# Latent attention: the order of turns, scores and root rows around the last gate tile

## The reference, cut to what matters

```python
yc = gla_mixer(gq, gk, gv, g_low, gr, ...)      # gated linear attention, 4 heads of 128
#   o = rms_norm(o, g_norm);  return o * silu(gr)
yd = mla_mixer(c_q, c_kv, k_r, ...)             # latent attention, 4 heads, causal, blocks of 128 queries
#   s = (q_nope k_nope + q_rope k_rope) * scale;  masked;  p = softmax(s);  o = p v
y = concatenate([yc, yd]) @ od_w_out
x = layer_norm(ALPHA * x + y, ...)
```

## Time and profile before

| | us |
| --- | --- |
| median of 3 runs | 2010.84 |
| lowest, highest | 2009.81, 2011.89 |
| profiled execution, its own time | 2011.19 |
| span of the profiled execution | 2009.4 |
| TensorE matmuls busy | 1965.6 (98% of the span) |
| VectorE, ScalarE, GpSimd busy | 935.4, 733.3, 344.2 |
| mean granted TensorE clock | 0.993 |

### The profile page before, as it was taken

How to read it: one execution, slowest core, us unless ns; L and a number is a source line. 1 busy time by engine, 2 the same in 40 slices (tenths; PEclk the granted TensorE clock), 3 DMA queues, 4 the chain that set the end, 5 groups by cost and what they waited for, 6 DMA issues and landing times.

```text
span 2009.4 us, 27314 instructions
## 1 busy us (share of the span) xinstructions
PE 1965.6 (98%) x11541; PEld 1188.6 (59%) x11541; DVE 935.4 (47%) x1254; ACT 733.3 (36%) x1173; POOL 344.2 (17%) x355
## 2 busy tenths in 40 slices
PE   8999999999999999999999999999999999999997
PEld 5655655757664444885568444448865585444476
DVE  6666686655543322244655222223555663222224
ACT  6444312445343431143534232212464543322213
POOL 1011111410132210033014121100400124212001
PEclk9999999999999999999999999999999999999999
DMA  7221200233322333322121232334111123322331
GB/s 245 84 84 60 68 22 21 87 123 105 105 69 100 105 105 105 106 85 103 59 97 59 89 102 103 105 105 137 53 64 45 40 85 105 104 88 101 105 105 43
DMA packets 28228, 179.66 MB, mean 89 GB/s; under 512 B 2960, under 2 KB 7184, under 8 KB 7184
## 3 DMA queue, kind: packets, MB, share of 16 engines
q1 hardware_dynamic: 27312, 170.93, 24.7%
q10 hardware_dynamic: 512, 4.94, 0.7%
q0 software_dynamic: 288, 2.10, 0.3%
HBM read 175.86 MB, written 2.10 MB: 89 GB/s over the span
## 4 chain that ended last, share of the span: by engine, by line
PE 90%; DVE 5%; ACT 2%; issue 1%; DMA 1%; POOL 1%; SPq 0%; ACTq 0%; DVEq 0%
PE psum_a L383 26%; PE psum_a L385 26%; PE psum_a L384 26%; PE psum_b L520 2%; PE psum_a L724 2%; PE psum_a L662 1%; DMA W<-weights 1%; DVE ARENA L1831 1%; PE psum_b L639 1%; PE psum_a L735 1%; ACT W_PARTS L1238 1%; PE psum_b L1063 1%; DVE W_PARTS L1812 1%; PE psum_a L704 1%; PE psum_a L851 1%
## 5 line engine op out<-in xcount | busy, mean ns | idle before, releaser
L1812 DVE SCALAR_TENSOR_TENSOR W_PARTS<-W,W_PARTS 128x2048 f16<-128x2048 f32 x138 | 316.1, 2294 | 583.6 <-ACT W_PARTS L1238 583.6
L383 PE MATMUL psum_a<-U,W_PARTS 128*128 128x512 f16 (+1 forms) x1240 | 465.9, 376 | 2.8 <-DVE U L1826 1.8
L384 PE MATMUL psum_a<-U,W_PARTS 128*128 128x512 f16 (+1 forms) x1240 | 465.7, 376 | 0.0
L385 PE MATMUL psum_a<-U,W_PARTS 128*128 128x512 f16 (+1 forms) x1240 | 465.5, 375 | 0.0
L1238 ACT ACTIVATE W_PARTS<-W 128x2048 f16<-128x2048 f32 x138 | 262.3, 1905 | 441.9 <-PE psum_a L385 440.1
L383 PE MATMUL psum_a<-ARENA,W_PARTS 128*128 128x256 f16 (+1 forms) x860 | 268.6, 312 | 1.9 <-DVE ARENA L2327 1.3
L385 PE MATMUL psum_a<-ARENA,W_PARTS 128*128 128x256 f16 (+1 forms) x860 | 268.6, 312 | 0.0
L384 PE MATMUL psum_a<-ARENA,W_PARTS 128*128 128x256 f16 (+1 forms) x860 | 268.6, 312 | 0.0
L383 PEld LDWEIGHTS psum_a<-U,W_PARTS 128*128 128x128 f16 x1240 | 121.5, 98 | 148.7 <-issue 5.1
L385 PEld LDWEIGHTS psum_a<-U,W_PARTS 128*128 128x128 f16 x1240 | 121.5, 98 | 141.8 <-issue 0.8
L384 PEld LDWEIGHTS psum_a<-U,W_PARTS 128*128 128x128 f16 x1240 | 121.5, 98 | 141.4 <-issue 3.5
(11 more groups left out here) (316 smaller groups left out, 2966.3 us busy)
## 6 DMA issues: line engine op xcount, KB each, us to landing
W<-weights SPq DMA_DIRECT2D x159, 1024.0 KB, 4.8
CON<-const ACTq DMA_DIRECT2D x1, 3071.5 KB, 11.2
X<-x_in SPq DMA_DIRECT2D x4, 256.0 KB, 3.8
X<-x_in SPq DMA_DIRECT2D x1, 1024.0 KB, 8.0
U<-dft POOLq DMA_DIRECT2D x1, 1024.0 KB, 5.3
ARENA<-dft POOLq DMA_DIRECT2D x1, 1024.0 KB, 5.2
U<-mem_in ACTq DMA_DIRECT2D x1, 1024.0 KB, 4.7
y_out<-U SPq DMA_DIRECT2D x2, 512.0 KB, 2.9
```

The costliest lines, as they stand in the source:

```text
L383: nc.tensor.matmul(out, left(0), right(0), start=first, stop=False)
L384: nc.tensor.matmul(out, left(0), right(1), start=False, stop=False)
L385: return nc.tensor.matmul(out, left(1), right(0), start=False, stop=last)
L1812: nc.vector.scalar_tensor_tensor(out=home[:, 1, :], in0=W[g % 2][:, :], scalar=W_SCALE, in1=home[:, 0, :], op0=ALU.mult, op1=ALU.subtract) ...
```

## The change

On TensorE the turns of block 1 and the scores of block 3 move into `gr1_after`, so that they stand ahead of the last gate tile. The root rows of heads 0 to 2 stand right behind that tile, then the turns of block 2, and the root row of head 3 behind those; `head_roots` gets the heads as a list for this. On ScalarE the exponentials of block 3 stand ahead of the copy of the last gate tile. On VectorE the normalising of block 3 stands between the scaling of the third head and that of the fourth. What is computed does not change.

```diff
@@ head_roots @@
                 pe.wait_ge(sem(f"{name}_inverse"), 1)
-                for h in range(heads):
+                for h in heads:
                     bank = reuse(R, ("rn", name, h))
                     nc.tensor.matmul(bank[:, :], back(h), rows, start=True, stop=True).then_inc(R.done, 1)
@@ -787,7 +787,7 @@
-            head_roots("hy", 4, ZT[0:64, 2, :], lambda ct: gback[:, ct, :], B)
+            head_roots("hy", range(4), ZT[0:64, 2, :], lambda ct: gback[:, ct, :], B)
@@ -1162,12 +1162,13 @@
                 row_turns(MLA, 0)
                 row_scores(MLA, 2, score_mla)
                 head_sums("gla", 4, lambda h: KS[:, h, :], one_row, G)
+                row_turns(MLA, 1)
+                row_scores(MLA, 3, score_mla)
 
             project_panel("gr", 1, U16, after=gr1_after)
-            row_turns(MLA, 1)
-            row_scores(MLA, 3, score_mla)
-            head_roots("gla", 4, RINV[0:64, :], row_back)
+            head_roots("gla", range(3), RINV[0:64, :], row_back)
             row_turns(MLA, 2)
+            head_roots("gla", (3,), RINV[0:64, :], row_back)
             for tt in range(4):
                 pe.wait_ge(A.freed_sem(("mv", tt)), A.freed_at(("mv", tt)))
             for b in range(3):
@@ -1774,8 +1775,8 @@
             root_rows("gla", ROOT[0:64, :], P, G)
             row_exps(MLA, 2)
             row_copies(MLA, 1)
+            row_exps(MLA, 3)
             gr_copy(3)
-            row_exps(MLA, 3)
             row_copies(MLA, 2)
             used(("gr", 1))
             row_copies(MLA, 3)
@@ -2559,7 +2560,8 @@
             row_norm(MLA, 2)
             for h in range(4):
                 scale_rows(("rn", "gla", h), OGL[:, h, :], OGL[:, h, :], par("gla_norm"))
-            row_norm(MLA, 3)
+                if h == 2:
+                    row_norm(MLA, 3)
             used(("gr", 1))
```

## The result

| | before | changed |
| --- | --- | --- |
| median of 20 executions, us | 2011.94 | 2015.01 |
| lowest to highest, us | 2009.78 to 2014.93 | 2011.92 to 2017.98 |
| ratio to before, 95% interval | | 1.0017, 1.0010 to 1.0023 |
| span of the profiled execution, us | 2009.4 | 2013.0 |
| mean granted TensorE clock in it | 0.993 | 0.991 |

The change costs 3.1 us by the medians, 0.17%. That is slower, though inside the 0.2% that the prediction called the same; the time of 2015.0 lies above the range, which ended at 2013.9. (The three executions known before had a median of 2010.84; with twenty it is 2011.94.)

What follows compares the result with a forecast made beforehand. TensorE is busy for 98% of the span, so only its stops can be won. New stops of 2.9 us less 2.3 gone cost 0.6, giving 2011.4 from the 2010.84 median; range 2008.7 to 2013.9.

Steps and rivals of the forecast that it cites:

- path: Time to the output projection without clock effects: 2.9 us of new stops against 2.3 gone, 0.6 us longer.
- T1: TensorE's turns of block 1's probabilities, ahead of the gate: start at 1565.44 after a new stop of 0.58 us.
- R3: Root row of the fourth head on TensorE: waits 0.3 us for the gate tile's bank, starts at 1579.3 at the earliest.
- om's fourth head: Head 3 of block 0's outputs on TensorE: waits 2.0 us for the fourth scaling, until 1582.9 against 1582.33.
- meeting of VectorE and GpSimd: Block 3's normalising beside GpSimd's products: two of four instructions held by the port lock, fourth scaling ends at 1582.85.
- Rival A: Fourth scaling isn't late, so the 1.4 us cover after R3 shrinks to nothing: -1.1, 2009.7; chance 0.15.
- How the numbers follow: Closing step: forecast of +0.6 us gets 0.58; same 0.92, slower 0.05, faster 0.03.
- Rival B: Half clock after the 2.0 us stop in block 0's outputs: 1.7 us lost, 2013.1; chance 0.15 once, 0.05 more.
- T3: TensorE's turns of block 3's probabilities, after the outputs of blocks 0 to 2: 1.9 us, waiting for nothing.
- Wrong would be: Signs against the forecast: normalising under 2 us, granted clock below 1 in the stretch, or output projection before 1593.5.
- its worse form: Rival B twice, with the upper end of the meeting: 4.8 us lost, 2015.6, slower by over 0.2%; chance 0.05.
- T2: TensorE's turns of block 2's probabilities: start at 1579.69 before; the 1.2 us stop ahead of them was to go.

Runs made afterwards that it cites:

- e3: Changed kernel with GpSimd's four products held back until block 3 is normalised; ratio to before 0.9998.
- e1: Changed kernel with its VectorE part undone, all four heads scaled before block 3 is normalised; ratio to before 0.9991.
- e5: e1 with dummy TensorE products in five stops outside the edited stretch; ratio to before 0.9971.
- e6: Kernel before, with dummy TensorE products in five stops outside the edited stretch; ratio to before 0.9981.
- e7: Changed kernel with dummy TensorE products in five stops outside the edited stretch; ratio to before 0.9979.
- b4: Kernel before, with four dummy TensorE products (0.86 us in all) ahead of the third gate tile; ratio to before 1.0005.
- e2: Changed kernel with six more TensorE products filling the stop between heads 2 and 3 of block 0's outputs; ratio to before 0.9998.
- e4: Kernel before, with only the VectorE part: block 3 normalised between the third and fourth scaling; ratio to before 1.0026.
- s4: Changed kernel with four dummy TensorE products ahead of the third gate tile, 0.86 us later; ratio to before 1.0012.
- s8: Changed kernel with eight dummy TensorE products ahead of the third gate tile, 1.73 us later; ratio to before 1.0016.

## Why the prediction was wrong

The path was right, nearly to the tenth:

| step | forecast | measured |
| --- | --- | --- |
| T1 | 1565.44 | 1565.36 |
| gate starts, no stop | 1569.9 | 1569.72 |
| R3 | 1579.3 | 1579.22 |
| normalising of block 3: start, length | 1578.8, 3.3 | 1578.74, 3.25 |
| the first two, the last two | 1.1 and 1.4, 0.8 | 1.04 and 1.49, 0.8 |
| fourth scaling ends | 1582.85 | 1582.65 |
| om's fourth head | 1582.9 | 1582.70 |
| path | +0.6 | +0.47 |

Two small things differ. The gate's copy was ready at 1578.7, half a microsecond earlier than forecast, so that R3 never waited for it (0.3 too much). The stop in om was 1.49 by the timeline; counted from start to start, as the 2.0 of the forecast was, it was 1.7. Neither moves the path: that stop is what is left until the fourth scaling ends, and the scaling came within 0.2 of its forecast. The chain that ended last in the changed kernel runs as the sum did: root rows, third scaling, the slow normalising, fourth scaling, om.

```profile
1577.87 0.75 DVE ARENA L2213
...
1578.74 3.25 DVE MIX L1962 x4
1581.99 0.67 DVE ARENA L2213
...
1582.70 6.55 PE psum_a L1137 x42
```

On the meeting of VectorE and GpSimd two of the four instructions were held, as the sum had it; e3 confirms it from the other side, 1.68 for all four without the meeting. The Trainium skill (SBUF — State Buffer, Who interferes with whom) lets a tensor_scalar enter the modes that use the port pair shared with GpSimd; whoever issues first then holds the pair for its whole instruction and the other is blocked. The trace agrees: 1.04 and 1.49 beside GpSimd, against 0.42 each in e3. Rival A is refuted for this kernel and true for e1 and e3, with its size: -1.05 against the -1.1 forecast.

What failed is the step "How the numbers follow", in two of its terms: the half clock behind the new stop, which the sum put at nothing, and the base. Rival B, one stretch of half clock on om and T3, was in both profiles of the changed kernel, with its place and nearly its price: 1.6 against 1.7. It is also what "Wrong would be" had named, a granted clock below 1 in this stretch. I gave B 0.20 with its worse form and made the case without it the likeliest.

The three in eight from the earlier trace rows was a count over stops of one execution. It was read as a chance that is drawn anew for each execution. But each stop has its own. Eleven profiles have the same TensorE program up to 1543 (all but e5, e6 and e7), and in them the stop of 1.31 near 1528 was followed by half clock in eleven, that of 1.67 near 989 in ten, that of 1.90 near 891 in eight, that of 1.65 near 272 in three and the four others in none. The place of the stops against the clock moves a little from execution to execution (the first stretch of half clock starts between 21.9 and 24.0 in thirteen of the fourteen profiles; e7 has none there), and mostly not enough to change the outcome. So a stop rather has its half clock in most executions or in few, and a likeliest case had to be chosen between the two, with B's time as an even rival. The earlier trace rows also shows the price too small for one of its three: the window behind the stop of 1.67 ends at 996, within the stretch, which lasts 6.82 and lost 3.4.

```profile
992.03:998.85 6.82, 6.82 (x30) 3.42 (x28) 5.09 (x6) 0.38 (x1) 0.00 (x0) 0.50 0.01 2
```

Then the base. I added the sum to 2010.84, the median of three. The kernel before scatters from 2007.7 to 2016.5 over all of its executions, with a mean of 2012.2, mostly since it loses between some 10 and 20 us to the clock. 1.1 of the 3.6 by which 2015.0 lies above 2011.4 is this. The rest is 1.6 of clock in the stretch, less 0.1 of path, and 1.0 that I can't place. The changed kernel's mean loss to the clock is 1.9 ± 0.5 above before, so one such stretch for nearly every execution would fill it; but both profiles of the changed kernel also show one near 1999 behind a stop of 1.58 that both kernels have, and b4 leaves room for a shift alone to move the mean by one. The mean of the rest is 0.8 ± 0.2 above before where the path is 0.47; that difference isn't explained either. How the 1.9 is divided between the new stop and the later ones stays open: it would take many more profiles of the same kernel. The range took 1.0 for the scatter of the base below and nothing for it above; with it the upper end would have been 2014.9, and B's own time 2014.2.

The ratio of 1.0017 is inside of the 0.2% that I called the same, at its edge, and its interval reaches beyond. That its direction is the one forecast is partly luck: the forecast had it from the path alone, which is 0.5 of the 3.1.

## What to carry to other kernels

Price a reordering by the stops of TensorE that it makes, not only by the sum of their lengths: the stops of the kernel before, none above 1.21, were cheaper than one of 1.49 in a place where it brought half clock. Where a stop of this size is new, give the time with half clock behind it as an equal case, and take the base from many executions. When such a stop can't be avoided, work of no use in it can be worth more than waiting (e2: 0.19% between two kernels of the same order). A VectorE instruction that is moved in front of a critical one must be priced at the new place, with what GpSimd does there: three lines moved were 1.5 us, and one wait on GpSimd gave them back.

## What the runs showed of the hardware

- The loss to the clock is most of what executions of one program differ by: the 31 executions of the kernel before that were timed beside e1 to e4 have a standard deviation of 1.9 us, and of 1.0 when (1 - clock) x span is taken off each.
- A stop of 1.49 us was followed by half clock in two profiles of the changed kernel and by full clock in three (s4, s8, e7). The stop of 1.2 ahead of T2 was followed by full clock in the kernel before and in b4, and by half clock in e4. In the eleven profiles with the same TensorE program up to 1543, one stop of 1.66 was never followed by it and one of 1.31 always. So length alone doesn't decide.
- Dummy work in stops lowered the mean loss to the clock by 6.8 ± 0.8 in e6 and by 2.8 ± 0.6 in e2. The Trainium skill (TensorE: Matmul & The Clock Gate, What's actually happening) has activity release the gate. These two numbers agree with it.
- Half clock that falls on a stretch in which TensorE would have waited anyway costs nothing: in e4 the turns of block 2 and the first six records of om took 3.69 against 2.46 in the kernel before, only to meet a stop of 2.70, and in e6 6.8 us less of it gave 3.5 us.
